# Two feed-forward layers: nine of eleven up groups as seven block products, weight sums by accumulating DMAs

## The reference

```python
def swiglu(x, w_gate, w_up, w_down):
    return (jax.nn.silu(x @ w_gate) * (x @ w_up)) @ w_down

    for l in range(DEPTH_2):
        x = x + 0.5 * swiglu(rms_norm(x, ffn1_norm[l]), ffn1_w_gate[l], ffn1_w_up[l], ffn1_w_down[l])
        ...
        x = x + 0.5 * swiglu(rms_norm(x, ffn2_norm[l]), ffn2_w_gate[l], ffn2_w_up[l], ffn2_w_down[l])
    return x
```

## Time and profile before

| | |
|---|---|
| median of 3 runs | 2365.07 us (2364.47 to 2366.45) |
| span of the profiled execution, first to last instruction | 2362.9 us |
| PE busy | 2328.1 us, 99% of the span |
| DVE, ACT, POOL busy | 1200.3, 878.0, 468.8 us (51%, 37%, 20%) |
| PE in the chain that ended last | 87% of the span |
| granted TensorE clock | 0.999 of full speed in the mean |

### The profile page before, as it was taken

How to read it: one execution, slowest core, us unless ns; L and a number is a source line. 1 busy time by engine, 2 the same in 40 slices (tenths; PEclk the granted TensorE clock), 3 DMA queues, 4 the chain that set the end, 5 groups by cost and what they waited for, 6 DMA issues and landing times.

```text
span 2362.9 us, 27596 instructions
## 1 busy us (share of the span) xinstructions
PE 2328.1 (99%) x11083; PEld 1893.2 (80%) x11083; DVE 1200.3 (51%) x1817; ACT 878.0 (37%) x1362; POOL 468.8 (20%) x475
## 2 busy tenths in 40 slices
PE   7999999999999999999999999999999999999999
PEld 5888877888787877777888888888887868888887
DVE  6555765555324456635545336444335984444423
ACT  4322345554223447733323234233225353323321
POOL 0111523445002048800000010000011870000000
PEclk9999999999999999999999999999999999999999
DMA  8664035656223210023233232333332212333322
GB/s 295 189 200 146 1 114 163 191 183 187 92 96 105 90 57 2 1 63 98 89 98 98 98 97 91 98 98 96 100 101 88 81 36 81 95 94 97 98 98 80
DMA packets 169333, 247.41 MB, mean 105 GB/s; under 512 B 14889, under 2 KB 110694, under 8 KB 169206
## 3 DMA queue, kind: packets, MB, share of 16 engines
q1 hardware_dynamic: 156276, 200.93, 26.5%
q0 software_dynamic: 12624, 44.54, 6.1%
q10 hardware_dynamic: 306, 0.19, 0.0%
HBM read 243.51 MB, written 2.10 MB: 104 GB/s over the span
## 4 chain that ended last, share of the span: by engine, by line
PE 87%; DVE 6%; POOL 3%; issue 2%; ACT 1%; DMA 1%; ACTq 0%; SPq 0%; POOLq 0%; DVEq 0%
PE ps L586 79%; DVE dsa_mask L2547 1%; POOL hg_k L2798 1%; PE ps L1050 1%; DVE w_lo L1957 1%; POOL nsa_p L2888 1%; PE ps L1066 1%; DVE small L2545 1%; DVE h_lo L2054 1%; PE ps L558 1%; PE ps L1040 0%; PE ps L1039 0%; PE ps L1281 0%; POOL nsa_b L2857 0%; PE ps L966 0%
## 5 line engine op out<-in xcount | busy, mean ns | idle before, releaser
L1957 DVE TENSOR_TENSOR w_lo<-w_raw,w_hi 128x1024 fp32r<-128x1024 f32 (+2 forms) x358 | 445.8, 1245 | 1004.7 <-ACT w_hi L1373 1004.4
L1373 ACT ACTIVATE w_hi<-w_raw 128x1024 fp32r<-128x1024 f32 (+2 forms) x364 | 380.7, 1046 | 1088.7 <-PE ps L586 1088.4
L586 PE MATMUL ps<-h_hi,w_hi 128*128 128x512 f32 (+1 forms) x1928 | 756.9, 393 | 4.9 <-DVE w_lo L1957 3.3
L586 PE MATMUL ps<-h_lo,w_hi 128*128 128x512 f32 (+1 forms) x1928 | 750.6, 389 | 0.0
L586 PE MATMUL ps<-h_hi,w_lo 128*128 128x512 f32 (+1 forms) x1928 | 750.4, 389 | 0.0
L586 PEld LDWEIGHTS ps<-h_hi,w_hi 128*128 128x128 f32 (+1 forms) x1928 | 361.3, 187 | 93.7 <-issue 7.6
L586 PEld LDWEIGHTS ps<-h_hi,w_lo 128*128 128x128 f32 (+1 forms) x1928 | 361.4, 187 | 76.4
L586 PEld LDWEIGHTS ps<-h_lo,w_hi 128*128 128x128 f32 (+1 forms) x1928 | 361.5, 187 | 75.9 <-issue 1.7
L586 PE MATMUL ps<-hid_hi,w_hi 128*128 128x512 f32 x616 | 240.9, 391 | 0.0
L586 PE MATMUL ps<-hid_lo,w_hi 128*128 128x512 f32 x616 | 239.7, 389 | 0.0
L586 PE MATMUL ps<-hid_hi,w_lo 128*128 128x512 f32 x616 | 239.7, 389 | 0.0
(11 more groups left out here) (397 smaller groups left out, 2570.0 us busy)
## 6 DMA issues: line engine op xcount, KB each, us to landing
w_raw<-in_ffn_w_up SPq DMA_DIRECT2D x264, 256.0 KB, 3.0
w_raw<-in_ffn_w_down SPq DMA_DIRECT2D x176, 256.0 KB, 2.8
m_raw<-in_ada_w POOLq DMA_DIRECT2D x80, 512.0 KB, 4.4
w_raw<-in_ffn_w_gate SPq DMA_DIRECT2D x88, 256.0 KB, 2.8
w_raw<-in_hg_w_in SPq DMA_DIRECT2D x64, 256.0 KB, 3.1
w_raw<-in_nsa_w_in SPq DMA_DIRECT2D x40, 256.0 KB, 2.9
w_raw<-in_w_in SPq DMA_DIRECT2D x32, 256.0 KB, 2.8
...
```

What stands on the lines that cost most here:

```text
L586: ins = K.nc.tensor.matmul(out, lhsT, rhs, start=start, stop=stop)
L1373: K.nc.scalar.activation(K.half(K.w_hi[u % SPL], width), K.half(K.w_raw[u % RAW], width), ACT.Copy) \
L1957: K.nc.vector.tensor_tensor(K.half(K.w_lo[u % SPL], width), K.half(K.w_raw[u % RAW], width), hi, ALU.subtract) \
```

## The change

In ffn_c and ffn_d the first two up groups stay as they are (`PLAIN_GROUPS`). The other nine take their gate and up products as one 2 x 2 block product. The weights of a group are four blocks of 512 input features x 256 output features: a11 and a12 of the gate matrix, a21 and a22 of the up matrix. The other operand is four blocks of 512 features x 256 tokens. Seven block products (`PRODUCTS`: p5, p1, p7, p6, p2, p4, p3, in this order) take the place of eight. A block product is one unit of 24 matmuls of 128 x 128 weights by 256 columns.

Four of the seven need a sum of weight blocks: s1 = a21 + a22, s2 = s1 + a11 and s4 = s2 + a12 are made one after the other in the buffer "chain"; s3 = a11 + a21 in the buffer "third". The first block of each is loaded by SyncE; the others are added in place by four DMAs with `accum_op=ALU.add` that GpSimd issues (`gpsimd_sums`). s2 is added once p5 has been split, s4 once p6 has been split. A group has five raw buffers, and there are two sets (`MORE_RAW`), so SyncE loads a group ahead. The split buffers are three (`FAST_SPL`), and the split of unit n + 3 stands in iteration n of ScalarE's and VectorE's programs, ahead of the work on product n.

The four sums of feature blocks (t1 to t4) are made and split once in each feed-forward, beside the two plain groups. PSUM takes four banks for a group, X, Y, Z and W; VectorE combines them (u2, u3, up1, gate0, up0, gate1, gate2, scaled) and gates. The hidden tiles are kept unsplit (`hid`), and each is split in both down halves into a ring of two buffers (`scalar_hid_high`, `vector_hid_low`).

The diff, cut to what the prediction speaks of:

```diff
@@ -323,14 +362,22 @@
                               for half, w in enumerate((gate_w, up_w))]
+            if tag in FAST:
+                for g in range(PLAIN_GROUPS, UP_GROUPS):
+                    for name, w, k in (("a11", gate_w, 0), ("a12", gate_w, 1), ("a21", up_w, 0), ("a22", up_w, 1)):
+                        self.blocks[tag, g, name] = w[512 * k:512 * k + 512, 256 * g:256 * g + 256].rearrange("(kk p) c -> p kk c", p=P)
+                    for name in ("a11", "third", "a12", "a22", "chain"):
+                        load((tag, g, name), [(slice(0, 4), slice(0, 256), self.blocks[tag, g, OPENS_WITH.get(name, name)])], fast_slot(g, name))
+                for g, product in fast_order():
+                    self.unit[tag, g, product] = unit(512, (tag, g, product), FAST_SPL)
+            self.unit[tag, "down"] = len(self.units)
             for half in halves_of(tag):
                 for pair in range(UP_GROUPS):
-                    units.append(([(kk, slice(0, 512), down_w[(2 * pair + kk) * P:(2 * pair + kk + 1) * P, half * 512:half * 512 + 512])
-                                   for kk in range(2)], 512))
+                    one([(kk, slice(0, 512), down_w[(2 * pair + kk) * P:(2 * pair + kk + 1) * P, half * 512:half * 512 + 512])
+                         for kk in range(2)])
         w = io["hg_w_in"][0]
         for n, base in (("f", D), ("q", 0), ("v", 2 * D), ("g", 3 * D)):
...
@@ -379,6 +451,39 @@
+FAST = ("ffn_c", "ffn_d")
+PLAIN_GROUPS = 2
+MORE_RAW = 6
+FAST_SPL = 3
+PRODUCTS = {"p5": ("s1", "t1", "Y"), "p1": ("a11", "b11", "X"), "p7": ("s3", "t3", "Z"), "p6": ("s2", "t2", "W"),
+            "p2": ("a12", "b21", "X"), "p4": ("a22", "t4", "Z"), "p3": ("s4", "b22", "Y")}
+OPENING = ("p5", "p1", "p7", "p6")
+WEIGHTS_IN = {"p5": "chain", "p6": "chain", "p3": "chain", "p7": "third"}
+OPENS_WITH = {"chain": "a21", "third": "a11"}
+LAST_READ = {"chain": "p3", "third": "p7", "a11": "p1", "a12": "p2", "a22": "p4"}
+def fast_order():
+    return [(g, p) for g in range(PLAIN_GROUPS, UP_GROUPS) for p in PRODUCTS]
+def fast_slot(g, name):
+    return ("chain", "third", "a11", "a12", "a22").index(name) + (0 if g % 2 else 5)
+def sum_signal(g, name):
+    return 2 * (g % 2) + (name == "third")
+def fast_bank(tag, g, role):
+    return up_banks(tag, g)["XYZW".index(role)]
...
+def raw_free(K, e, key, before):
+    if type(key) is tuple and key[1] == PLAIN_GROUPS:
+        e.wait_ge(*K["unit_multiplied"].at(K.unit[key[0], 0] - 1))
+    if type(before) is tuple:
+        tag, g, name = before
+        e.wait_ge(*K["w_low"].at(K.unit[tag, g, LAST_READ[name]]))
+    elif before is not None:
+        e.wait_ge(*w_low(K, before))
...
@@ -880,7 +1019,7 @@
             pe.wait_ge(*K["mod_ready"].at("mod13"))
         for pair in range(UP_GROUPS):
             u, final = K.unit[tag, "down"] + h * UP_GROUPS + pair, pair == UP_GROUPS - 1
-            pe.wait_ge(*K["hid_low"].at((tag, pair, 1)))
+            pe.wait_ge(*K["hid_low"].at((tag, h * UP_GROUPS + pair) if tag in FAST else (tag, pair, 1)))
             pe.wait_ge(*K["w_low"].at(u))
...
+FREED_BY = {"X": "gate0", "Y": "gate1", "Z": "up0", "W": "u2"}
+def tensor_fast_up(K, tag, emptied):
+    pe, ps = K.pe, K.ps
+    for g, product in fast_order():
+        u, (_, feature, role) = K.unit[tag, g, product], PRODUCTS[product]
+        bank, opens = fast_bank(tag, g, role), product in OPENING
+        if g < PLAIN_GROUPS + 2:
+            emptied(g - 2)
+        elif opens:
+            pe.wait_ge(*K["up_part"].at((tag, g - 2, FREED_BY[role])))
+        if product == "p2":
+            pe.wait_ge(*K["first_copied"].at((tag, g)))
+        elif not opens:
+            pe.wait_ge(*K["up_part"].at((tag, g, "up1" if product == "p3" else "u3")))
+        if feature.startswith("t"):
+            pe.wait_ge(*K["feature_low"].at((tag, feature)))
+        pe.wait_ge(*K["w_low"].at(u))
+        hi, lo = K.hi(u), K.lo(u)
+        for kt in range(4):
+            m_hi, m_lo = K.moving(feature, kt)
+            for f in range(2):
+                out, w = ps[:, bank, f * 256:f * 256 + 256], slice(kt * 256 + f * P, kt * 256 + (f + 1) * P)
+                K.nc.tensor.matmul(out, hi[:, w], m_hi, start=opens and kt == f == 0, stop=False, skip_group_check=True)
+                K.nc.tensor.matmul(out, hi[:, w], m_lo, start=False, stop=False, skip_group_check=True)
+                ins = K.nc.tensor.matmul(out, lo[:, w], m_hi, start=False, stop=kt == 3, skip_group_check=True)
+        ins.then_inc(*K["unit_multiplied"].up(u))
...
@@ -1366,11 +1539,14 @@
     if u >= len(K.units):
         return
     act = K.act
-    act.wait_ge(*K.raw_landed[u % RAW].at(u))
-    if u >= SPL:
-        act.wait_ge(*K["unit_multiplied"].at(u - SPL))
-    width = K.units[u][1]
-    K.nc.scalar.activation(K.half(K.w_hi[u % SPL], width), K.half(K.w_raw[u % RAW], width), ACT.Copy) \
+    width, fast = K.units[u]
+    if fast is not None and fast[2] in WEIGHTS_IN:
+        act.wait_ge(*K.sum_landed[sum_signal(fast[1], WEIGHTS_IN[fast[2]])].at((*fast[:2], PRODUCTS[fast[2]][0])))
+    else:
+        act.wait_ge(*K.raw_landed[K.raw_slot(u)].at(u if fast is None else (*fast[:2], PRODUCTS[fast[2]][0])))
+    if K.slot_before[u] is not None:
+        act.wait_ge(*K["unit_multiplied"].at(K.slot_before[u]))
+    K.nc.scalar.activation(K.half(K.hi(u), width), K.half(K.raw(u), width), ACT.Copy) \
         .then_inc(*K["w_high"].up(u))
...
+def scalar_features(K, tag, u):
+    before = PLAIN_BEFORE[tag]
...
+    for name in {5: ("t1",), 6: ("t3", "t2"), 7: ("t4",)}.get(u, ()):
+        K.act.wait_ge(*K["feature_made"].at((tag, name)))
+        K.nc.scalar.activation(K.feat[name][:, :, 0, :], K.feat_raw[name][:, :, 1, :], ACT.Copy).then_inc(*K["feature_high"].up((tag, name)))
+def scalar_fast_up(K, tag):
+    nc, act, order, first = K.nc, K.act, fast_order(), K.unit[tag, PLAIN_GROUPS, "p5"]
+    def gate(g):
+        act.wait_ge(*K["up_part"].at((tag, g, "gate2")))
+        nc.scalar.activation(K.gate_buf[:, :, :], K.gate_buf[:, :, :], ACT.Silu).then_inc(*K["silu"].up((tag, g)))
+    scalar_split(K, first + 2)
+    for n, (g, product) in enumerate(order):
+        if n + 3 < len(order) + SPL:
+            scalar_split(K, first + n + 3)
+        if product == "p1":
+            act.wait_ge(*K["unit_multiplied"].at(first + n))
+            if g > PLAIN_GROUPS:
+                act.wait_ge(*K["up_part"].at((tag, g - 1, "gate1")))
+            nc.scalar.activation(K.u2[:, :, :], K.ps[:, fast_bank(tag, g, "X"), :].rearrange("p (f t) -> p f t", f=2), ACT.Copy) \
+                .then_inc(*K["first_copied"].up((tag, g)))
+        elif product == "p3":
+            gate(g)
+        if g == UP_GROUPS - 1 and product in ("p2", "p4"):
+            scalar_hid_high(K, tag, int(product == "p4"))
+def scalar_hid_high(K, tag, n):
+    pair, act = n % UP_GROUPS, K.act
+    if n < 2:
+        act.wait_ge(*K["unit_multiplied"].at(K.unit[tag, UP_GROUPS - 1, ("p5", "p7")[n]]))
+    else:
+        act.wait_ge(*K["unit_multiplied"].at(K.unit[tag, "down"] + n - 2))
+    act.wait_ge(*K["hid_gated"].at((tag, pair, 1) if pair < PLAIN_GROUPS else (tag, pair)))
+    K.nc.scalar.activation(K.ring_hi[n % 2][:, :, :], K.hid[:, 2 * pair:2 * pair + 2, :], ACT.Copy).then_inc(*K["hid_high"].up((tag, n)))
...
+def vector_features(K, tag, u):
+    nc, dve, raw = K.nc, K.dve, K.features_raw
...
+            .then_inc(*K["feature_low"].up((tag, name)))
+    if u == 4:
+        made("t1", raw[:, 0:4, early], raw[:, 0:4, late])
+    elif u == 5:
+        made("t3", raw[:, 0:4, late], raw[:, 4:8, late])
+        dve.wait_ge(*K["feature_made"].at((tag, "t3")))
+        made("t2", raw[:, 0:4, early], K.feat_raw["t3"][:, :, 1, :])
+        low("t1")
+    elif u == 6:
+        dve.wait_ge(*K["feature_made"].at((tag, "t2")))
+        made("t4", raw[:, 4:8, early], K.feat_raw["t2"][:, :, 1, :])
+        low("t3")
+    elif u == 7:
+        dve.wait_ge(*K["feature_high"].at((tag, "t2")))
+        low("t2")
+        low("t4")
...
+def vector_fast_up(K, tag):
...
+    def bank(g, role):
+        return K.ps[:, fast_bank(tag, g, role), :].rearrange("p (f t) -> p f t", f=2)
+    def gated(g):
+        dve.wait_ge(*K["silu"].at((tag, g)))
+        dve.wait_ge(*part(g, "scaled"))
+        nc.vector.tensor_tensor(two(g), two(g), gate_buf[:, :, :], ALU.mult).then_inc(*K["hid_gated"].up((tag, g)))
+    order = fast_order()
+    vector_split(K, first + 2)
+    for n, (g, product) in enumerate(order):
+        if n + 3 < len(order) + SPL:
+            vector_split(K, first + n + 3)
+        if product == "p5" and g > PLAIN_GROUPS:
+            gated(g - 1)
+        elif product == "p7" and before == "ffn_b" and g - PLAIN_GROUPS < KD:
+            vector_final_x(K, g - PLAIN_GROUPS)
+        dve.wait_ge(*K["unit_multiplied"].at(first + n))
+        if product == "p6":
+            dve.wait_ge(*K["first_copied"].at((tag, g)))
```

(53 more changed lines are left out.)

189 lines of the change are left out of this document (150 added, 39 removed).

## The result

| | before | changed |
|---|---|---|
| median | 2365.49 us (4 runs) | 2435.85 us (2429.97 to 2438.58, 4 runs) |
| ratio | | 1.0296 [1.0281, 1.0312] |
| span of the profiled execution | 2362.9 us | 2433.5 us |
| granted TensorE clock, mean | 0.999 | 0.985 |

What follows compares the result with a forecast made beforehand. PE was taken to bound the kernel. A period of 23.1 us against 21.76 gives 24 us over 18 groups, plus 2 for the entries: 2365.07 + 26 = 2391 us, range 2351 to 2428 us, the forecast's own 2370 to 2417.

Steps and rivals of the forecast that it cites:

- Pace of the products: TensorE's block products: 0.119 us per 256-column matmul, 20.0 us a group of seven, 31 us less for 18 groups.
- First circle: p4 waits for u3, VectorE's chained step on p6: stall 1.17 us a group, least period 21.2 us.
- Second circle: Loop through s4's adding DMA, the splits, u2, u3, p4 and p3: period 17.0 + L, 23.1 us.
- L: Time from issue to landing of s4's accumulating DMA: 6.1 us, as 4.4 plus 1.7 for a second pass.
- The clock: TensorE's clock in the stalls of some 1 to 3 us before p4: not expected to fall.
- The entries: From group 1 into the first block product's splits: about 1 us for each feed-forward, 2 in all.
- DMA engines: Load on the DMA engines: 15.3 to 22.1 us of transfers in a group of about 22, share 0.7 to 0.9.
- What was costed at nothing: Other sums' landings, GpSimd's issue, feature sums, the down units' extra split steps and ffn_c's rescaling: all hidden.
- quick landing: Rival: s4's sum lands with L at or below 4.4 us, only the first circle counts, 2357 us; chance 0.27.
- no change: Rival: L between 4.6 and 5.1 us, total within 5 us of the median; chance 0.11.
- slow matmuls: Rival: 256-column matmuls take 0.16 us each, a group 26.9 us, +92 us; chance 0.02.
- full DMA engines: Rival: landings queue, L passes 7.5 us; 2425 us at L = 8, 2442 at 8.9; chance 0.13.

Runs made afterwards that it cites:

- e4: Changed kernel with VectorE's split for p3 in iteration p6 moved behind u2, u3 and up1: 2360.68 us, 0.9978.
- e8: e6 with e7's move of the silu behind the split for p6: 2347.65 us, 0.9923.
- e2: Changed kernel without the accumulating DMA that makes s4; p3 multiplies s2 instead: 2373.73 us, 1.0033.
- e1: Changed kernel with 24 matmuls that nothing reads placed ahead of p4's wait in each block-product group: 2409.59 us, 1.0189.
- e3: Changed kernel with GpSimd's four DMAs a group overwriting their targets instead of adding: 2376.61 us, 1.0046.
- e5: e4 with the splits for the third and fourth block product moved ahead of plain group 1's scaling and gating: 2350.16 us, 0.9936.
- e6: e5 with SyncE holding the first down loads until s2 of the last group has landed: 2351.13 us, 0.9934.
- e7: Changed kernel with ScalarE's silu of a group moved behind the split for p6 of the next group: 2410.9 us, 1.018.

## Why the prediction was right in its mechanism and wrong in its size

- **Pace of the products: right.** 0.119 us a matmul was forecast, 0.120 measured (e4, e8). The gain is 18 x (21.76 - 20.16) = 29 us for the 31 that it promised, and e8 has 18 of it.
- **First circle: right.** Forecast 1.17 us of stall and a period of 21.2; e2 shows 1.20 from start to start, and a period of 21.34, 1.18 above the products' 20.16.
- **Second circle and L: right.** s4's landing to ScalarE took 6.2 us (forecast 6.1), the stall before p4 2.9 to 3.3 in 15 of 18 groups (forecast 3.1), released by u3 on VectorE, and the split of p3 was released by the landing. With the clock kept (e1) the period is 23.2 to 23.4 us in the mean against 23.1. e3 and e4, which take away the adding and the order, each remove it.
- **The clock: this step failed.** "or if the clock falls in the stalls, which at some 1 to 3 us before p4 I do not expect: the clock is 1.00 in all four stages now". The reason given was no reason: in the kernel before PE was never idle in those stages, so the earlier trace rows could not tell what a stall does to the clock. It falls behind 15 of the 18, for 26.3 us (e1). The case had no chance of its own: the chances add to 1 over L and the pace alone. The trace of before had something to say on it, outside the four stages. Besides the wait at its very start it holds three idle stretches of 1.9 to 2.4 us by their rows; here are two of them, each with a window behind it or around it:

```profile
17.08 0.67 PE L500 MATMUL ps<-const,vec_rows 68*128 68x68 f32 x3 [2.36 <-DMA vec_rows<-in_ffn_conv_b]
...
1830.31 0.47 PE L586 MATMUL ps<-w_hi,h_hi 128*128 128x512 f32 x1 [2.02 <-ACT relu L1805]
```

```profile
16.90:20.10 3.20, 3.02 (x6) 1.54 (x7) 2.48 (x2) 0.48 (x1) 0.00 (x0) 0.50 1.01 411
1826.00:1834.00 8.00, 5.98 (x30) 4.49 (x29) 7.48 (x13) 5.13 (x8) 2.37 (x1) 1.00 0.29 90
```

The clock fell to half behind the first and stayed full behind the second, as behind the third (1943.62). The second kept it in the changed kernel and in e1 as well, and lost it in the other seven kept traces, though the stretch is the same 2.0 us: one trace is one draw. So a fall was possible, and its direction was known, since a slower clock only adds to a stall. The rows behind the stalls now give the size: 3.4 us at 0.213 us a matmul hold 16 matmuls, which take 1.9 us at 0.120: 1.5 us lost each time.
- **The entries: mis-sized.** "about 1 us for each feed-forward, 2 in all". The gating of the plain group was seen, but not summed: 2.35 + 3 x 1.28 us of VectorE work lie ahead of a split whose product is due two short products after the entry. They are stalls of 4.1 us each, and the low clock behind them; e5 gave back 10.5 us for the two.
- **DMA engines: right.** 15.3 to 22.1 us of work a group were forecast, and a share of 0.7 to 0.9; it is 0.77 and 0.82. They are not the bound, even at 1.05 (e4).
- **What was costed at nothing: right, but for the step into the down parts and the last group.** The stall ahead of the first down product loses 1.5 us in each feed-forward. Behind it the down parts cost 0 and 0.9 us. s2 came in time in the changed kernel; once the groups were faster, s2 or s4 of a last group landed late, each time with down loads issued 1.4 to 4.1 us before it (e4, e6, e8).

The sum: 70 us are 18 x (23.3 - 21.76) = 28 for the circle, 26 for the clock in the groups, 10.5 for the entries by e5, 3 for the steps into the down parts, and 1 in the down parts; 1 or 2 were not taken apart. In place of these terms the forecast had 24, 0, 2, 0 and 0.

Some sums of the prediction are slightly off by its own formulas, none of them in the forecast itself. With L = 4.4 the second circle is still the longer one (21.4 us), so quick landing gives 2361 us and not 2357. At 0.111 us a matmul 2357 comes at L = 4.6 and not 4.8, and L = 4.4 gives 2353 and not 2351. L between 4.4 and 4.9, and not 4.6 to 5.1, keeps the total within 5 us of the median, and L = 5.1 gives 2373 where the forecast's own range begins at 2370.

The rivals: quick landing and no change are out by L, slow matmuls by the pace, and full DMA engines would have given a similar total (2425 to 2442) by a wrong mechanism; e1 and e4 tell it apart. The Trainium skill (TensorE: Matmul & The Clock Gate, Why this matters for your kernels) advises against idle gaps of over about 3 us between bursts of matmuls. By that rule the forecast's stall of 3.1 us stood at the edge and deserved a chance of its own, and the traces are stricter: in e7 stalls of 1.9 to 2.4 us were followed by half clock in 7 of 14 cases.
